# Giving each activation operand of a 16,128-matmul chain its own SBUF distance from the weights

## What is computed

```python
def first_block(x, mem, ...):
    x = layer_norm(x, emb_ln_g, emb_ln_b)
    for l in range(2):
        h = hybrid_mixer(x, w_in[l], ...)            # x @ w_in (7680 columns), attention, 3 branches, gates
        x = layer_norm(alpha * x + h, ...)
        h = memory_cross_attention(x, mem, xa_q[l], xa_kv[l], xa_o[l])
        x = layer_norm(alpha * x + h, ...)
        u, gt = split(x @ ffn_w_in[l])               # 1024 -> 2 x 2816
        h = (silu(dwconv(gt) + b) * u) @ ffn_w_out[l]
        x = layer_norm(alpha * x + h, ...)
def second_block(x, ...):
    for l in range(2):
        x = x + 0.5 * swiglu(rms_norm(x), gate, up, down)    # 1024 -> 2816 -> 1024
        h = rms_norm(x) @ w_in_2[l]                  # pooling, two attentions, a convolution
        x = x + mix @ w_out_2[l]
        x = x + 0.5 * swiglu(rms_norm(x), gate2, up2, down2)
    return rms_norm(x)
```

## Time and profile before

| | us |
|---|---|
| median of 3 executions | 2274.64 |
| lowest, highest | 2267.52, 2275.7 |
| the profiled execution | 2269.32 |
| its span, first to last instruction | 2267.5 |

### The profile page before, as it was taken

One profiled execution on the slowest core, in us unless ns is written; L12 is line 12 of the kernel. 1 busy time (PEld: TensorE's weight loads), 2 busy tenths in 40 slices (PEclk: granted clock), 3 DMA queues, 4 the chain that ended last, 5 costly groups with the idle time before them and its releaser, 6 DMA issues.

```text
span 2267.5 us, 39445 instructions
## 1 busy us (share of the span) xinstructions
PE 2138.3 (94%) x17460; PEld 2080.3 (92%) x17460; DVE 1436.8 (63%) x1690; ACT 1009.3 (45%) x1166; POOL 99.7 (4%) x69
## 2 busy tenths in 40 slices
PE   7999999899899999989997999879999999979998
PEld 6899999899899999989997999769999999868997
DVE  5665554666765656457776756866666666765665
ACT  4544454444445443544444434334444444234443
POOL 1000010100100000010001000001000000000000
PEclk9999999999999999999998999989999999989999
DMA  5444543355444455435552554323554555213542
GB/s 198 148 162 163 204 162 143 133 185 189 149 149 165 146 188 191 152 112 216 186 189 104 199 192 175 112 75 135 204 203 149 209 200 186 112 68 115 209 186 94
DMA packets 52858, 366.08 MB, mean 161 GB/s; under 512 B 5904, under 2 KB 5904, under 8 KB 9296
## 3 DMA queue, kind: packets, MB, share of 16 engines
q1 hardware_dynamic: 52272, 361.21, 43.3%
q0 software_dynamic: 416, 2.35, 0.3%
HBM read 362.49 MB, written 1.05 MB: 160 GB/s over the span
## 4 chain that ended last, share of the span: by engine, by line
PE 76%; DVE 10%; issue 9%; ACT 3%; POOL 1%; DMA 0%; POOLq 0%; ACTq 0%; DVEq 0%
PE accM L989 43%; PE scoreP L989 17%; PE outP L989 8%; PE turnP L989 7%; DVE wlo L1317 2%; DVE yc L1704 1%; ACT whi L728 1%; PE turnP L1176 1%; DVE xl L1335 1%; ACT ew L909 1%; DVE acc L1350 1%; PE outP L1203 0%; DVE cen L1395 0%; DVE cen L1401 0%; DVE mrs L1646 0%
## 5 line engine op out<-in xcount | busy, mean ns | idle before, releaser
L1317 DVE TENSOR_TENSOR wlo<-raw,whi 128x2048 fp32r<-128x2048 f32 x325 | 744.1, 2290 | 411.5 <-ACT whi L728 411.0
L728 ACT ACTIVATE whi<-raw 128x2048 fp32r<-128x2048 f32 x336 | 640.4, 1910 | 256.4 <-PE accM L989 169.9
L989 PE MATMUL accM<-xh,whi 128*128 128x256 f32 x1152 | 338.9, 294 | 16.8 <-DVE xl L1415 10.9
L989 PE MATMUL scoreP<-xh,whi 128*128 128x256 f32 x1152 | 325.9, 283 | 17.8 <-DVE xl L1415 9.0
L989 PE MATMUL accM<-xl,whi 128*128 128x256 f32 x1152 | 324.9, 282 | 0.0
L989 PE MATMUL accM<-xh,wlo 128*128 128x256 f32 x1152 | 324.9, 282 | 0.0
L989 PE MATMUL scoreP<-xl,whi 128*128 128x256 f32 x1152 | 323.7, 281 | 0.0
L989 PE MATMUL scoreP<-xh,wlo 128*128 128x256 f32 x1152 | 323.5, 281 | 0.0
L989 PE MATMUL accM<-fh,whi 128*128 128x256 f32 x1056 | 293.2, 278 | 0.7 <-DVE wlo L1317 0.7
L989 PE MATMUL accM<-fh,wlo 128*128 128x256 f32 x1056 | 293.1, 278 | 0.0
L989 PE MATMUL accM<-fl,whi 128*128 128x256 f32 x1056 | 293.1, 278 | 0.0
(11 more groups left out here) (264 smaller groups left out, 4297.2 us busy)
## 6 DMA issues: line engine op xcount, KB each, us to landing
raw<-in_W SPq DMA_DIRECT2D x336, 1024.0 KB, 4.8
biasr<-in_bias SPq DMA_DIRECT2D x16, 256.0 KB, 2.7
raw<-in_memT SPq DMA_DIRECT2D x2, 1024.0 KB, 4.7
cc<-in_consts POOLq DMA_DIRECT2D x1, 1536.0 KB, 6.7
x<-in_xT SPq DMA_DIRECT2D x4, 256.0 KB, 4.4
out<-x SPq DMA_DIRECT2D x4, 256.0 KB, 2.5
c<-in_consts SPq DMA_DIRECT2D x1, 464.5 KB, 6.1
par<-in_par POOLq DMA_DIRECT2D x2, 203.5 KB, 3.7
```

Source lines behind the costliest of these rows:

```text
L728: nc.scalar.activation(whi[:, slot(c), :], raw[:, n % RING, :], ACT.Copy).then_inc(split_hi.sem, 1)
L989: return nc.tensor.matmul(dst, a, b, start=start, stop=stop, skip_group_check=True)
L1317: v.tensor_tensor(wlo[:, slot(c), :], raw[:, n % RING, :], whi[:, slot(c), :].bitcast(F32), ALU.subtract).then_inc(split_lo.sem, 1)
```

## The change

Only the sizes of the unused tiles change, and three of them are new. No instruction is added, removed or moved: on every engine the same instructions stand in the same order, with other addresses. The tiles then start at these distances from the weights, modulo 512 bytes:

| operand | plain form before | after |
|---|---|---|
| `x` | 192 | 256 |
| `f` | 192 | 64 |
| `z` | 320 | 128 |
| `y`, `mem` | 192 | 320 |
| `m`, `o` | 192 | 384 |

Tiles that lie behind them in the same region move along: those of the attentions and gates by 128 bytes, `macc` by 192, and those of the second block (`cc` to `yc2`) by -128. `raw`, `whi`, `wlo`, the fp32 stream `x` itself, the constants, the parameters and `sq` to `otok` stay.

```diff
         x = sb("x", [P, KT, S])
-        _lead = sb("lead", [P, 48])
+        _lead = sb("lead", [P, 64])
         xh = sb("xh", [P, KT, S], F32R)
         xl = sb("xl", [P, KT, S], F32R)
-        _trail = sb("trail", [P, 80])
+        _trail = sb("trail", [P, 64])
...
         part1 = ExitStack()
+        _lead_y = sb("lead_y", [P, 32], where=part1)
         yh = sb("yh", [P, 3, 4, S], F32R, part1)
...
         mrg = ExitStack()
+        _lead_m = sb("lead_m", [P, 16], where=mrg)
         mh = sb("mh", [P, KT, S], F32R, mrg)
...
         xat = ExitStack()
+        _lead_mem = sb("lead_mem", [P, 32], where=xat)
         memh = sb("memh", [P, KT, S], F32R, xat)
...
-        _skip4 = sb("skip_mem", [P, 24 * 256], where=oxs)
+        _skip4 = sb("skip_mem", [P, 24 * 256 + 48], where=oxs)
         oh = sb("oh", [P, KT, S], F32R, oxs)
...
-        _lead_f = sb("lead_f", [P, 120], where=ff)
+        _lead_f = sb("lead_f", [P, 88], where=ff)
         fh = sb("fh", [P, 2, 2, S], F32R, ff)
...
-        _lead_z = sb("lead_z", [P, 96], where=ff)
+        _lead_z = sb("lead_z", [P, 80], where=ff)
         zh = sb("zh", [P, KT, S], F32R, ff)
```

## The result

The changed kernel takes 2328.1 us in the median of four executions (2326.42 to 2329.09), against 2273.1 us of the kernel before in the same comparison (four executions, 2267.52 to 2275.7). The ratio is 1.0229, with a 95% interval of 1.019 to 1.0268: slower by 55 us, well clear of the noise, and 16 us beyond the upper end of the predicted range. The profiled execution took 2327.19 us, 57.9 more than that of before.

The account below looks back on a forecast made before the run. It took TensorE's matmul cadence, 117.7 or 113.3 ns, as the bound. Terms 20.4 - 3.9 - 1.3 + 3.0 = +18.2 us on the profiled 2269.3 us gave 2287.5, say 2288 us; range 2236 to 2312.

Parts of the forecast that it names:

- What bounds the kernel: TensorE, busy 94% of the span: an address change matters only through how fast matmuls follow each other.
- Two cadences, set by interruptions, and 192 open to both: Matmuls start 117.7 or 113.3 ns apart; at distance 192 an interruption sets which, and it stays; 4.4 ns per matmul.
- first rival: All products: everything relevant turns fast, with 256 and 64 avoiding what makes 117.7 ns; 2240 to 2250 us, chance 0.21.
- x to 256: Plain `x` matmuls: 15% fast at 256, taken nearer to 320 than to 192; +20.4 us, bounds -16 and +27.
- the last rival: Plain `x` at 256: a third, higher cadence of 122 ns if its read meets the next weights' twice; 2336 us, chance 0.09.
- f to 64: `f` matmuls in the networks: all fast, moving away from 320; -3.9 us, at worst +9.7.
- m and o to 384: `m` and `o` matmuls: lose the fast cadence beside 320; +3.0 us, other end -0.4.
- z to 128: `z` matmuls: some 300 of 384 slow ones turn fast on leaving 320; -1.3 us, at worst 0.4.
- y: `y` matmuls moved to 320: already slow, so 0, at best -2.5 us.
- mem: `mem` matmuls moved to 320: plain may lose what swapped gains, at most 0.8 us each; together 0.
- Swapped x: `x` as stationary operand, at -256, which is 256 again: stays as slow as it is; 0, at best -3 us.
- The rule of the pages: Skill pages: only the VectorE-GpSimd port pair contends, TensorE's reads are independent; by that the whole sum would be 0.

Follow-up runs that it names:

- the scans: Two runs of the kernel before with each operand given its own distance (the second at odd multiples of 32 bytes): 2313.85 us and 2312.92 us.
- the shifted weights: Kernel before with `raw`, `whi`, `wlo` and `x` 64 bytes further on, the other activations at their old addresses: 2283.9 us.

## Why the prediction was wrong

**What bounds the kernel: right.** TensorE's cadence was the only thing that moved; DVE, the transfers and the clock stayed.

**Two cadences, set by interruptions, and 192 open to both: right in the main.** Both cadences stand at 192 in the kernels whose `x` is there, and at 448 in the one with all there. But a wait is not the only thing that sets one: an operand at 120.0 ahead does too, and in two runs the cadence changed at a border between equal distances without a wait. (Among the reasons for its first rival the prediction has 113.3 in the last four networks; it is the second and the last three, the third being slow from 1279 us on the earlier trace rows.)

**x to 256: the step that failed.** I weighed 256 between its neighbours and let the bounds be the two cadences that the trace had, so that the most it could lose was 27 us. There was a third, 120.0 ns, on the unbroken stretches of `x` in both forms. In the plain form: 9,792 x (119.9 - 115.1) = +47 us, against my +20.4. (Added up matmul by matmul over the traces it is +42, since those beside the small steps lose less.) Had every operand but `x` gone as badly as my bounds allow, and `x` to 117.7 throughout, the time would still have been about 2310, inside the range: it is the third cadence that left it. The neighbours say nothing about 256, since the price does not vary smoothly with the distance. The nearest thing was the last rival, a further step for `x`, to which I gave 122 ns, 2336 us and a chance of 0.09: right in its kind and 8 us off, with a step of 2.2 ns over 117.8 instead of 4.4; its reason, reads that meet twice, no run shows. I left its case outside the range as unseen, while "no row shows 256" was a reason to take it in.

**f to 64: wrong in sign.** I expected 113.3 on a slope away from 320. But 64 and 320 are the same distance modulo 256, so the three slow groups at 320 were already rows of 64. Term: +9.8 instead of -3.9.

**m and o to 384:** +3.9 (118.7 and 119.0 against 113.4 and 114.1), against +3.0. **z to 128:** +0.5 instead of -1.3. **y:** 0, as said. **mem:** swapped -0.9, where I had at most 0.8, and plain `mem` did not lose it again (115.5 after 115.6). **Swapped x:** +1.4 (119.6 against 117.6) instead of 0.

The terms as measured: 47 + 9.8 + 3.9 + 0.5 + 1.4 - 0.9 = 62 us, against 61.5 more busy time on the page. That they agree so well is partly luck, since each spreads the cadence of unbroken stretches over all matmuls of an operand. Added up matmul by matmul the terms are +42.4 for plain `x`, +9.9 for `f`, +3.5 for swapped `x`, +3.7 for `m` and `o`, +1.3 for `z`, -0.5 for `mem`, and +1.0 for all other steps. The profiled executions differ by 57.9, since TensorE's idle time fell by 3.6.

**The rule of the pages.** The rows: one and the same stream of matmuls runs at 113.3, 117.8, 118.7 or 120.0 ns, at full clock and without a wait, by the distance of its two operands (the scans and the shifted weights) and, at 192, by what went before. The Trainium skill, "SBUF — State Buffer", section "Who interferes with whom", has contention only on the port pair of VectorE and GpSimd. By that a change of addresses alone costs nothing, and the measured 55 us decide against it; whether TensorE's two reads hinder each other, the runs do not show. "TensorE: Matmul & The Clock Gate", section "Back-to-back issue gap", the Trainium skill again, gives 262 cycles, 109 ns, for 256 columns, as the gap of a matmul without a weight load in its budget. No steady stretch of products, each with its own weight load, came closer than 113.3 in any of the kernels.

## What to carry to other kernels

Where float32r matmuls of 256 columns with a new 128x128 weight load each run back to back, look at the distance between the moving and the stationary operand modulo 256 bytes, and measure a few distances instead of interpolating: here the cadence of an operand in the networks is between 113.3 and 120.4 ns with it, and 8 bytes can matter as much as 64. Two durations of one group in equal stretches (276 and 281 ns) without any wait were the sign of it here. And when a sum rests on a value that no row shows, its bounds are not the ends of what was seen so far.

## What the hardware showed that was not expected

- The cadence depends on the distance modulo 256 bytes: 120.0 ns at 0, 117.8 at 64 (113.3 in parts of `mem`, `o` and `z`), 118.5 to 119.0 and uneven at 128, 113.3 or 117.7 at 192; off these multiples it does not settle (116.7 to 120.4 in the mean).
- The sign counts: exchanging the moving and the stationary operand turns 192 into 64, and the cadence goes with it: swapped `x` has 117.6 in the mean with `x` at 192 and 115.9 with `x` at 64.
- At 192 two cadences, 113.3 and 117.7, hold for over a hundred microseconds with the same instructions and addresses; a network is 7 us longer in the slow one. Six matmuls at distance 256 led to the fast one at all eight places; four did at eight of nine and once turned the fast one into the slow one.
- What in SBUF or TensorE makes these values was not measured; the runs show the distance as the cause and not the mechanism behind it.
